# One split of weights moved ahead of a norm's root and reciprocal in a two-block transformer kernel

## What is computed

```python
# first block, its last lines
h = rmsnorm(x, norm_pre_ffn)
f = jnp.square(jax.nn.relu(h @ w_ff1)) @ w_ff2
x = x + rmsnorm(f, norm_post_ffn)
# second block, its first lines
h = jnp.concatenate([meta_tokens, x], axis=1)          # 16 + 256 tokens
u = rmsnorm_2(h, norm_mix_w)
z, xbc, dt_raw, conf_in = jnp.split(u @ w_in_2, ...)   # widths 1024, 2048, 16, 2048
# conf_in gives a gated convolution, xbc a state-space mixer that is gated with silu(z)
```

## Time and profile before

| | us |
|---|---|
| median of 3 runs | 1446.21 (1444.99 to 1447.1) |
| the profiled execution's own time | 1440.79 |
| its span | 1439.0 |
| TensorE matmuls, busy in the span | 1388.2 (96%) |
| VectorE busy | 1068.2 (74%) |
| ScalarE busy | 734.2 (51%) |

### The profile page before, as it was taken

One profiled execution on the slowest core, in us unless ns is written; L12 is line 12 of the kernel. 1 busy time (PEld: TensorE's weight loads), 2 busy tenths in 40 slices (PEclk: granted clock), 3 DMA queues, 4 the chain that ended last, 5 costly groups with the idle time before them and its releaser, 6 DMA issues.

```text
span 1439.0 us, 25238 instructions
## 1 busy us (share of the span) xinstructions
PE 1388.2 (96%) x10470; PEld 1274.9 (89%) x10470; DVE 1068.2 (74%) x1750; ACT 734.2 (51%) x1072; POOL 3.0 (0%) x9
## 2 busy tenths in 40 slices
PE   6999899998899999999999999999999999999997
PEld 6977799997899878999999999999987777888886
DVE  7754766446699998688999886888879888555554
ACT  6744655444556865676444445344443444444443
POOL 0000000000000000000000000000000000000000
PEclk9999999999999999999999999999999999999999
DMA  7423366554454301555665555555555555666563
GB/s 262 150 85 103 103 188 186 184 177 130 153 178 154 89 16 43 177 176 149 190 190 184 178 195 173 165 162 162 162 172 166 162 170 166 186 185 202 188 189 104
DMA packets 63618, 228.60 MB, mean 159 GB/s; under 512 B 7312, under 2 KB 8208, under 8 KB 63376
## 3 DMA queue, kind: packets, MB, share of 16 engines
q1 hardware_dynamic: 63072, 226.25, 50.7%
q10 hardware_dynamic: 432, 0.74, 0.1%
HBM read 225.91 MB, written 1.05 MB: 158 GB/s over the span
## 4 chain that ended last, share of the span: by engine, by line
PE 88%; DVE 7%; ACT 3%; issue 1%; DMA 0%; DVEq 0%; ACTq 0%
PE ps L327 17%; PE ps L329 17%; PE ps L328 17%; PE ps L930 9%; PE ps L932 8%; PE ps L931 8%; PE ps L894 2%; PE ps L648 2%; DVE W L1450 1%; DVE RSI L1456 1%; DVE plain L1705 1%; PE ps L377 1%; ACT W L967 1%; PE ps L379 1%; PE ps L523 1%
## 5 line engine op out<-in xcount | busy, mean ns | idle before, releaser
L1450 DVE TENSOR_TENSOR W<-raw,W 128x1024 fp32r<-128x1024 f32 x423 | 515.3, 1222 | 279.1 <-ACT W L967 278.8
L967 ACT ACTIVATE W<-raw 128x1024 fp32r<-128x1024 f32 x423 | 446.2, 1057 | 401.5 <-PE ps L932 208.4
L327 PE MATMUL ps<-XH,W 128*128 128x256 f32 (+1 forms) x1552 | 441.6, 285 | 1.6 <-DVE hid L1902 0.7
L328 PE MATMUL ps<-XL,W 128*128 128x256 f32 (+1 forms) x1552 | 439.1, 283 | 0.0
L329 PE MATMUL ps<-XH,W 128*128 128x256 f32 (+1 forms) x1552 | 436.7, 281 | 0.0
L327 PEld LDWEIGHTS ps<-XH,W 128*128 128x128 f32 x1552 | 291.3, 188 | 3.5 <-issue 1.5
L329 PEld LDWEIGHTS ps<-XH,W 128*128 128x128 f32 x1552 | 293.3, 189 | 0.0
L328 PEld LDWEIGHTS ps<-XL,W 128*128 128x128 f32 x1552 | 291.9, 188 | 0.0
L930 PE MATMUL ps<-W,HH 128*128 128x512 f32 x512 | 205.6, 402 | 0.8 <-ACT hid L1415 0.8
L932 PE MATMUL ps<-W,HL 128*128 128x512 f32 x512 | 203.0, 396 | 0.0
L931 PE MATMUL ps<-W,HH 128*128 128x512 f32 x512 | 202.9, 396 | 0.0
(11 more groups left out here) (345 smaller groups left out, 1967.3 us busy)
## 6 DMA issues: line engine op xcount, KB each, us to landing
raw<-in_w_dn SPq DMA_DIRECT2D x128, 512.0 KB, 3.6
raw<-in_w_up SPq DMA_DIRECT2D x128, 512.0 KB, 3.6
raw<-in_w_ff SPq DMA_DIRECT2D x64, 512.0 KB, 3.9
raw<-in_w_in SPq DMA_DIRECT2D x57, 512.0 KB, 3.7
raw<-in_w_out SPq DMA_DIRECT2D x24, 512.0 KB, 3.5
raw<-in_w_q SPq DMA_DIRECT2D x16, 512.0 KB, 3.7
raw<-in_w_kv SPq DMA_DIRECT2D x4, 512.0 KB, 3.6
plain1a<-in_memT SPq DMA_DIRECT2D x1, 1024.0 KB, 10.8
```

The source lines that it names most:

```text
L327: e.matmul(out, wh, xh, start=first, stop=False, skip_group_check=shared)
L328: e.matmul(out, wh, xl, start=False, stop=False, skip_group_check=shared)
L967: e.activation(W[:, u % NSLOT, 0, :], raw[:, u % NRAW, :], ACT.Copy).then_inc(s["hi"], 1)
L1450: e.tensor_tensor(W[:, u % NSLOT, 1, :], raw[:, u % NRAW, :], W[:, u % NSLOT, 0, :], ALU.subtract).then_inc(s["lo"], 1)
```

## The change

Four numbers on ScalarE and two on VectorE grow by one. With them one split more is issued in front of the root and of the reciprocal, and every later split of this place moves up by one position.

```diff
@@ ScalarE
-            hi_to(U_ZA + 4)
+            hi_to(U_ZA + 5)
             root(N_IN2, 5, 272, 1.0 / 1024, eps5)
-            hi_to(U_ZA + 5)
+            hi_to(U_ZA + 6)
             e.wait_ge(s["tmeta"], 2)
             for c, _ in enumerate(h_high(1, T2, 272, U_F2)):
                 if c in (1, 3, 5, 7):
-                    hi_to(U_ZA + 6 + c // 2)
+                    hi_to(U_ZA + 7 + c // 2)
@@ VectorE
-            lo_to(U_ZA + 4)
+            lo_to(U_ZA + 5)
             inverse(N_IN2, 272)
...
                 if c in (2, 4, 6, 8):
-                    lo_to(U_ZA + 4 + c // 2)
+                    lo_to(U_ZA + 5 + c // 2)
```

## The result

The changed kernel is faster: a median of 1436.91 us over 6 runs (1433.81 to 1439.23) against 1445.6 us over 6 runs of the kernel before (1444.11 to 1447.1). The ratio is 0.9945, with a 95% interval of 0.9933 to 0.9958, which is 8.0 us less (6.1 to 9.7).

A forecast was written before the change was run, and what follows sets the result against it. TensorE was taken as the bound, holding 88% of the chain, with waits on VectorE's splits. Losses 2.74 + 1.66 + 2.07, less 0.17, gave 6.30 us off the median 1446.21: 1439.9 us, range 1437.6 to 1443.7.

The forecast's parts named there:

- z4's split is free in front of root and reciprocal: z4's copy fits ScalarE's 3.18 us idle, its subtraction VectorE's 1.88; cost nothing, root and reciprocal keep their times.
- the rival of the held copy: z4's copy waits for slot or tile until z2 ends, delaying root and reciprocal; gain 4.8 us, 1441.4; chance 0.10.
- The later splits arrive in time: Splits of z5, z6, z7 and g0 move up one place, each ready before TensorE wants it.
- tightest link: z5 on TensorE: wanted from 366.27, its subtraction ready at 366.10, 0.17 us to spare.
- g1 is late next, by 0.2: g1's subtraction, behind four L1696 on VectorE, ends at 378.09; g1 starts at 378.14, 0.2 us late, 6.30 sooner than before.
- Gap A: TensorE's wait between z3 and z4: z4 could start at 363.41 and came at 366.15, 2.74 us lost.
- slow clock: Granted clock 0.64 in the stretch 366.1 to 370.8, while z4 to z7 run; 1.66 us lost.
- gap B: TensorE's wait between z7 and g0: g0 could start at 379.25 and came at 381.32, 2.07 us lost.
- less 0.17: Deduction from the summed losses, because g0 to g1 takes 3.29 us after the change and not 3.12.
- The first rival: The fall of the clock behind z4's wait is not in every run; without it gain 4.6 us, 1441.6; chance 0.27.
- It is carried to the end: Downstream work is fed by the gated units and starts sooner with them, so the 6.3 us reach the end unchanged.
- the last two rivals: Gain absorbed by VectorE from 400 to 500, 1446.2, chance 0.07; root starved behind z4's late tile, 1449.1, chance 0.04.

The follow-up runs named there:

- the run with two steps: The change carried one step further, z4 and z5 split ahead of root and reciprocal, later splits up again; ratio 0.996 to the kernel before.
- The runs with one half each: The change without moving g0's subtraction: ratio 0.9993 to the kernel before; the kernel before with only g0's subtraction moved ahead of L1688 to L1696: 0.9984.
- the two comparisons: The changed kernel against the kernel before, measured twice: ratio 0.9945 first, 0.9952 when repeated on one chip.

## Why the prediction was right

- *z4's split is free in front of root and reciprocal.* Right: root and reciprocal at the same 0.66 and 1.18 behind L342, with idle time left in front of them. The tile had landed and z1 was done; the rival of the held copy fell.
- *The later splits arrive in time.* Right down to the tightest link: z5 was given 0.17 to spare and started without idle. (The loads that go earlier are five and not four, since the subtractions of z4 to g0 each release one; no wait at the place names a load.)
- *g1 is late next, by 0.2.* It started 3.10 behind g0, where the run with two steps, in which its split is earlier, has 3.00: 0.1. The sum gave this step 3.29, so it had 0.19 too much here.
- *Gap A 2.74, slow clock 1.66, gap B 2.07, less 0.17: 6.30.* 6.40 against the trace that the sum was made for. The 0.19 too much at g1 is partly taken back by z4 to z7, which took 11.52 and not 11.44. The runs with one half each show how the terms hang together: gap B does not go with gap A, and without its own move it grows.
- *The slow clock.* The first rival was the one that mattered, and it was told too simply. I set the fall as either there or not, behind gap A alone, because the earlier trace rows show 1.00 behind gap B. The runs show falls behind either gap, so the term is 0, some 1.5 or some 3.1, not 1.66 or 0, and the guess that 2.58 is near the edge and 1.91 short of it was wrong: behind 1.9 the clock fell in 3 of 7. Without a fall the gain is 22.86 - 17.95 = 4.9, with two 8.0. That the one trace shown held one fall, close to the mean, was luck. The mean over four traces of the kernel before is a gain of 24.0 - 17.95 = 6.1; the two comparisons have 8.0 and 6.9, whose intervals hold 6.1 to 6.4.
- *It is carried to the end.* Nothing takes it up: from g1's first matmul to the end both kernels take 1054.5 to 1054.7, and the comparisons show no less than the place. Neither of the last two rivals happened.

The median taken off the runs shown was the weaker part: by it the forecast was 1439.9. Of the two medians measured, 1438.56 is within the range and 1436.91 is 0.7 below its low end. The medians of the first comparison differ by 8.7, more than its ratio gives (8.0) and more than the mean of the traces at the place (6.1); the traces put differences of this kind ahead of the place, where the arrival at the first L342 varies from 342.8 to 349.6.

## What to carry to other kernels

When an engine waits for a result with others' work still to be issued behind it, look for work that is ready in front of that wait, and check slot, tile and consumer of every step that moves up with it: here the second gap closed only because the last of them moved too, and the two moves were worth 2.3 and 2.2 alone. How far ahead is set by what the moved work itself must wait for; one split moved ahead cost nothing, two delayed the root without harm, three ate the slack of the tiles. A single trace can hold a stretch at the low clock that the next one lacks, here 1.5 us each, so take several before pricing one. And compare two traces by a distance inside them that begins ahead of the change, not by their spans.

## What was not expected

The same program has a different number of stretches at half clock from one execution to the next, far from the change too. The kernel before in its first trace and in the second, both at 50 to 60 us, where TensorE is busy all the time:

```profile
50.00:60.00 10.00, 10.00 (x89) 10.00 (x88) 7.94 (x11) 9.12 (x13) 0.00 (x0) 1.00 0.35 108
```

```profile
50.00:60.00 10.00, 10.00 (x69) 10.00 (x68) 7.34 (x9) 9.11 (x13) 0.00 (x0) 0.74 0.31 102
```

The second one lost clock at 50 to 70 and at 80 to 90 us as well, came to L342 at 349.56 instead of 342.96, and took 1446.64 us instead of 1440.79. That difference of 5.9 is nearly that of the arrival, 6.6, so it arose ahead of this place (up to the L342 behind z2 come 0.8 more, and the place itself, without a fall, takes 1.5 less); it is of the size by which runs of one kernel differ (5.4 among the six of the changed kernel). Why the clock falls there in one execution and not in another was not tried.
